# Stick-breaking attention without mask products: GpSimd selects the zeros, scores run ahead of the values

## The chip, the cores and the metric

The kernel runs on one core of one Trainium2 chip, as one launch. The metric is the device time of that launch in microseconds (us); lower is better.

## What is computed

The program is a chain of two transformer blocks on 256 tokens of width 1024, all in float32. Only one layer matters here: the stick-breaking attention of the first block's second layer, with 12 heads of 64 columns. Cut to what matters:

```python
z = einsum("bhqd,bhkd->bhqk", q, k) * scale          # 12 heads, 256 queries, up to 256 keys
mask = key_position < query_position                 # strictly causal
log_not = where(mask, log_sigmoid(-z), 0.0)
later = cumsum(log_not, axis=3, reverse=True) - log_not
wts = where(mask, exp(log_sigmoid(z) + later), 0.0)
out = einsum("bhqk,bhkd->bhqd", wts, v)
```

So the mask is needed twice: masked keys must add nothing to the running sums of log_not (which is minus the softplus of z), and their weights must be zero.

## The kernel before, in words

Every engine has its own instruction list, written by hand; semaphores (`wait_ge`, `then_inc`) order them against each other. TensorE (PE) runs nearly the whole time: most of the program is matmuls of weight matrices that are split into a high and a low part (by ACT at line 489 and DVE at line 966), multiplied in three passes.

The stick-breaking stage works through six **pairs** of heads, p = 0 to 5; the two heads of a pair (e = 0, 1) sit in partitions 0 to 63 and 64 to 127 of the transposed queries `qTB` and keys `kTB`. Everything is held transposed: keys in the partitions, queries in the columns. A head has 384 columns of a PSUM bank: columns 0 to 127 are key block 0 against query block 0, 128 to 255 key block 0 against query block 1, 256 to 383 key block 1 against query block 1. Three sets of two banks (`SB_BANK`) rotate over the pairs. The first and the last of the three blocks are the diagonal ones that need a mask. For one pair the steps are:

1. `sb_scores(p)` on PE. Per head, one product of the identity with `sb_neg_r` (line 2017) writes -1e30 at the masked places of both diagonal blocks and 0 elsewhere; three products of keys and queries of 128 columns each (lines 2022, 2026, 2030) add the scores to it. `sb_neg_r` is a rounded copy of a constant, made once by ACT (line 731).
2. `sb_negated(p)` on DVE (line 1221): -|z| of each head into `sbE`.
3. `sb_softplus(p)` on ACT: Exp (lines 742, 750), then Ln with bias 1 (lines 743, 755), in place in `sbE`.
4. `sb_plus(p)` on DVE (line 1229): max(z, 0) + `sbE` into `sbL`, the softplus; it is 0 at masked places, because z is -1e30 there.
5. `sb_sums(p)` on PE (lines 2038, 2040, 2042): products of `sbL` with a triangle and with ones, added onto the scores in PSUM, head by head. Each head's sums wait for its `sbL`.
6. `sb_weights(p)` on ACT (line 762): one Exp over both heads into `sbW`, the weights; masked places give exp of -1e30, which is 0.
7. `sb_values(p)` on PE (lines 2053, 2056): weights times values; then `sb_hi` on ACT (line 555) and `sb_lo` on DVE (line 1053) split the result into its two parts for the output product.

`sbE`, `sbL` and `sbW` are double buffered (`p % 2`). PE's order is written out by hand:

```python
for p in range(5):
    sb_sums(p)
    if p == 1:
        pe.wait_ge(s_qkd, 3)
    if p:
        sb_values(p - 1)
    if p + 2 < 6:
        sb_scores(p + 2)
```

After it come the first memory logits (line 1841), the sums of pair 5, and then pieces of the output product between the last values. ACT goes, for each p, `sb_softplus(p + 1)`, `sb_weights(p)`, `sb_hi(p - 1)`; DVE goes `sb_plus(p + 1)`, `sb_negated(p + 2)`, `sb_lo(p - 1)`. GpSimd (POOL) has nothing to do in this stage: its work before it is a table of 16 rows near the start, its work after it a DMA that waits for the next feed-forward layer.

Of the kernel before, what the change touches and what calls it, by code (L numbers as in the profile page):

```python
# [15 lines left out]
S = 256  # L16
D = 1024
P = 128
# [68 lines left out]
def build(nc, A):  # L87
# [3 lines left out]
    with ctx:  # L91
        def sem(name):
            return ctx.enter_context(nc.semaphore(name))
# [5 lines left out]
        def place(name, cols, dt=fp32, at=None):  # L99
            if at is None:  # L100
                at = plan["at"]
                plan["at"] += cols
            return nc.alloc_sbuf_tensor_at(name, [P, cols], dt, offset=first + 4 * at)
# [10 lines left out]
        ident_r = place("ident_r", P, f32r)  # L114
# [26 lines left out]
        def over(name, cols):  # L141
# [24 lines left out]
        sbE = over("sbE", 2 * 2 * 384)  # L166
        sbL = over("sbL", 2 * 2 * 384)
        sbW = over("sbW", 2 * 2 * 384)
        sb_neg_r = place("sb_neg_r", 2 * P, f32r, at=cur["at"])
        cur["at"] += 2 * P  # L170
        memPB = over("memPB", 4 * 512)

        cur["at"] = r1
# [27 lines left out]
        s_ohi, s_olo = sem("pair_hi"), sem("pair_lo")  # L201
        s_z, s_abs, s_sbe, s_sbl, s_tri, s_wt, s_sbpv = (sem(n) for n in ("sb_scores", "sb_negated", "sb_log1p",
            "sb_softplus", "sb_summed", "sb_weights", "sb_mixed"))
        s_neg, s_qkd, s_ptd = sem("sb_mask_rounded"), sem("qk_copied_dve"), sem("probsT_copied_dve")
        s_sg, s_hb, s_ht, s_hhi, s_hlo = (sem(n) for n in ("gate_act", "hidden", "hidden_transposed",
                                                         "hidden_hi", "hidden_lo"))
        s_x2p, s_x2h, s_x2, s_gel, s_cmpp, s_cmpc = (sem(n) for n in ("cmp_tokens", "cmp_hi", "cmp_lo",
# [38 lines left out]
        def bank(b, lo=0, hi=512):  # L246
            return ps[:, b, lo:hi]
# [17 lines left out]
            return t[:, (u % NRAW) * UNIT:(u % NRAW + 1) * UNIT]  # L265

        sb_tri, sb_ones = sbc[:, 0:P], sbc[:, P:2 * P]
        sb_neg = sbc[:, 512:1024].rearrange("p (z n) -> p z n", z=2)[:, :, P:2 * P]


        ssq, var, t1, t2 = tiny[:, 0:4], tiny[:, 4:6], tiny[:, 6:8], tiny[:, 208:210]
# [140 lines left out]
        @block.gpsimd  # L412
        def _(pool):
            nc.gpsimd.memset(ident[:, :], 1.0).then_inc(s_idn, 1)
            pool.wait_ge(s_idn, 1)
            nc.gpsimd.affine_select(ident[:, :], ident[:, :], [[1, P]], ALU.is_equal, 0.0, base=0, channel_multiplier=-1)\
                .then_inc(s_idn, 1)
            pool.wait_ge(s_mm, U0["mem_a"])
            pool.dma_start(relT[0:16, :], A["rel_bias_2"].rearrange("n h -> h n"), allow_slow_non_contiguous=True).then_inc(s_tin, 16)
            nc.gpsimd.memset(stage[0:16, 0:512], NEG).then_inc(s_tab, 1)  # L420
            pool.wait_ge(s_tab, 1)
            pool.wait_ge(s_tin, 16)
            for n, (lo, hi) in enumerate(BUCKETS):
                nc.gpsimd.tensor_copy(stage[0:16, TABLE_J0 + lo:TABLE_J0 + hi],
                                      relT[0:16, n:n + 1].broadcast_to([16, hi - lo])).then_inc(s_tab, 1)
            pool.wait_ge(s_tab, 1 + len(BUCKETS))
            pool.dma_start(A["table"], stage[0:16, 0:512]).then_inc(s_tabd, 16)

            pool.wait_ge(s_mm, U0["b_down"] + 1)
            pool.wait_ge(s_hlo, 22)  # L430
            pool.dma_start(gfin[:, :], A["final_norm"].partition_broadcast(P)).then_inc(s_gfin, 16)
            pool.wait_ge(s_mm, U0["b_down"] + 11)

            pool.wait_ge(s_tabd, 16)
            pool.dma_start(strip[:, :].rearrange("p (h c) -> p h c", h=16),
                           bass.AP(A["table"].tensor, 0, [[1, P], [512, 16], [1, 384]])).then_inc(s_strip, 16)
            pool.dma_start(caus[:, :], A["causal"]).then_inc(s_strip, 16)
            for n, kv in enumerate(("k", "v")):
                pool.dma_start(per[16 * n:16 * n + 16, :], A[f"cmp_pe_{kv}_2"].rearrange("(j r) d -> j (r d)", r=2))\
                    .then_inc(s_ind, 16)  # L440
                pool.dma_start(w2[:, HD * n:HD * n + HD], A[f"cmp_w2_{kv}_2"]).then_inc(s_ind, 16)

            def copied(dst, src, step, n):

                s_, d_ = both(front, W_FRONT, src, 1), both(dup, 768, dst, P)
                nc.gpsimd.tensor_copy(d_.rearrange("p t (z n) -> p t z n", n=n),
                                      bass.AP(s_.tensor, s_.offset, [s_.ap[0], s_.ap[1], [step, P // n], [1, n]]))\
                    .then_inc(s_dup, 1)
            pool.wait_ge(s_gact, emptied(G0["front"] + 1, "act"))
            copied(X_KC, C_KC + HD, -HD, HD)  # L450
            copied(X_VC, C_VC + HD, -HD, HD)
            pool.wait_ge(s_gact, emptied(G0["front"] + 2, "act"))
            copied(X_KA, C_KA, 0, HD)
            copied(X_KI, C_KI, 0, 32)
            copied(X_KS, C_KS + HD, -HD, HD)
            pool.wait_ge(s_gact, emptied(G0["front_rest"], "act"))
            copied(X_KW, C_KW + HD, -HD, HD)
            pool.wait_ge(s_sel, 1)
            for h in range(8):
                if h == 6:  # L460
                    pool.wait_ge(s_m, A0["nsa"] + 16)
                for T, (lo, hi) in enumerate(CAUSAL):
                    b0 = 384 * h + TABLE_J0 + 128 * T
                    ins = nc.gpsimd.tensor_tensor(sel_strip(h, lo, hi), strip[:, b0:b0 - (hi - lo):-1], sel[:, lo:hi],
                                                  ALU.add)
                ins.then_inc(s_selb, 1)
            pool.wait_ge(s_mm, U0["down2"] + 1)
            pool.wait_ge(s_hlo, 29)
            pool.dma_start(gfin[:, :], A["norm_final_2"].partition_broadcast(P)).then_inc(s_gfin, 16)
# [3 lines left out]
        def _(act):  # L473
# [253 lines left out]
            act.wait_ge(s_half, HALF["q"] + 1)  # L727
            empty_group(G0["q"], both(qB, D, 0), "b_mix")
            act.preload_act_table_set("natural_log_exp_and_others")
            act.wait_ge(s_sbc, 16)  # L730
            A_(sb_neg_r[:, :].rearrange("p (z n) -> p z n", z=2), sb_neg, ACT.Copy).then_inc(s_neg, 1)
            q_copy(6, ch(qTB, 0, 2), 4, HD ** -0.5)
            act.wait_ge(s_mm, U0["q"] + 4)
            empty_group(G0["q"] + 1, both(qB, D, 512), "b_mix")
# [829 lines left out]
        def _(pe):  # L1564
# [445 lines left out]
            def sb_scores(p):  # L2010

                c = S * p
                if p >= 3:
                    pe.wait_ge(s_wt, p - 2)
                banks = [SB_BANK[p % 3] + e for e in range(2)]
                for e in range(2):
                    MM(bank(banks[e], 0, 512).rearrange("p (z n) -> p z n", z=2)[:, :, 0:P], ident_r[:, :],
                       sb_neg_r[:, :].rearrange("p (z n) -> p z n", z=2), start=True, stop=False,
                       skip_group_check=True)
                for e in range(2):  # L2020
                    r = slice(64 * e, 64 * e + 64)
                    MM(bank(banks[e], 0, P), kTB[r, c:c + P], qTB[r, c:c + P], start=False, stop=False,
                       skip_group_check=True)
                for e in range(2):
                    r = slice(64 * e, 64 * e + 64)
                    MM(bank(banks[e], P, S), kTB[r, c:c + P], qTB[r, c + P:c + S], start=False, stop=False,
                       skip_group_check=True)
                for e in range(2):
                    r = slice(64 * e, 64 * e + 64)
                    MM(bank(banks[e], 256, 384), kTB[r, c + P:c + S], qTB[r, c + P:c + S], start=False, stop=False,  # L2030
                       skip_group_check=True).then_inc(s_z, 1)

            def sb_sums(p):

                for e in range(2):
                    b = SB_BANK[p % 3] + e
                    pe.wait_ge(s_sbl, 2 * p + e + 1)
                    MM(bank(b, 0, 256), sb_tri, sb_half(sbL, p, e, 0, 256), start=False, stop=False,  # L2038
                       skip_group_check=True)
                    MM(bank(b, 128, 256), sb_ones, sb_half(sbL, p, e, 256, 384), start=False, stop=False,  # L2040
                       skip_group_check=True)
                    MM(bank(b, 256, 384), sb_tri, sb_half(sbL, p, e, 256, 384), start=False, stop=True,
                       skip_group_check=True).then_inc(s_tri, 1)

            def sb_values(p):

                o = O0["sb"] + p
                pe.wait_ge(s_wt, p + 1)
                pe.wait_ge(s_olo, o - 1)
                outs = [ps[64 * e:64 * e + 64, OB + o % 2, 0:S] for e in range(2)]  # L2050
                for e in range(2):
# [4 lines left out]
                    ins = MM(outs[e][:, P:S], tok(kvB, 2 * SB, 1)[:, v0:v0 + HD], sb_half(sbW, p, e, 256, 384),  # L2056
                             start=False, stop=True)
                ins.then_inc(s_sbpv, 1)
            pe.wait_ge(s_neg, 1)
            pe.wait_ge(s_idr, 1)  # L2060
            pe.wait_ge(s_qkc, 7)
            sb_scores(0)
            pe.wait_ge(s_qkd, 1)
# [17 lines left out]
            for p in range(5):  # L2081
                sb_sums(p)
                if p == 1:
                    pe.wait_ge(s_qkd, 3)
                if p:
                    sb_values(p - 1)
                if p + 2 < 6:
                    sb_scores(p + 2)
            pe.wait_ge(s_wt, 4)
            mem_logits("mem_b", 0, qTB[:, 6 * S:8 * S], mkTB)  # L2090
            sb_sums(5)
# [451 lines left out]
```

## Time and profile before

| | us |
|---|---|
| median of three runs | 954.84 (954.49 to 955.57) |
| the profiled execution, its own time | 954.67 |
| its span | 953.0 |
| PE busy | 944.5 (99% of the span) |
| DVE busy | 622.1 (65%) |
| ACT busy | 514.6 (54%) |
| POOL busy | 30.7 (3%) |
| TensorE clock, mean share of full speed | 0.999 |

How to read it: the chain of work that ended last is 98% PE, so a microsecond that PE saves or waits is, to first order, a microsecond of the run. The stick-breaking stage lies between 338.5 and some 370 us of the span. A plain float32 product shows as two matmul records (so "x2" on lines 2022 to 2056 is one product), while the mask product of line 2017, in the rounded format, shows as one. Records of neighbouring matmuls overlap; the time that a step takes PE is therefore read from the start of its first record to the start of the next step's first record.

### The profile page before, as it was taken

The page shows a single profiled execution, that of the slowest core. Times are in us where ns is not written, and L with a number is a line of the kernel's source. Part 1 is how long each engine was busy: PE and PEld are TensorE (multiplying, and loading weights), DVE is VectorE, ACT ScalarE, POOL GpSimd, SP SyncE. Part 2 cuts the span into 40 slices and gives each one's busy share as a digit, 9 for nine tenths or more (in the row PEclk, how much of TensorE's full clock was granted, in tenths as well). Part 3 has the DMA queues.
Part 4 walks back from the last instruction along what each step waited for, and adds up shares of the span by engine and source line. Part 5 has one row for each costly group of instructions (what it writes and reads, how often), then busy time and mean ns, then how long its engine had stood idle before and what let it go on. Part 6 is the DMA issues. An engine that isn't in the chain of part 4 may idle for free.

```text
span 953.0 us, 13086 instructions
## 1 busy us (share of the span) xinstructions
PE 944.5 (99%) x5102; PEld 784.9 (82%) x5102; DVE 622.1 (65%) x858; ACT 514.6 (54%) x687; POOL 30.7 (3%) x71
## 2 busy tenths in 40 slices
PE   9999999999999999999999999999999999999997
PEld 6878888888888887888888888877777888888886
DVE  6554877776457366577777447688884776775444
ACT  6754555554346575655555336667685455544333
POOL 0400000000000000000000001000310000000000
PEclk9999999999999999999999999999999999999999
DMA  9715555555555420655555657643224555555561
GB/s 363 234 50 187 189 181 197 196 176 184 215 177 178 175 89 1 221 177 183 202 188 176 220 199 302 220 145 134 89 99 167 177 177 180 189 200 203 188 209 44
DMA packets 25723, 168.66 MB, mean 177 GB/s; under 512 B 2749, under 2 KB 3627, under 8 KB 6475
## 3 DMA queue, kind: packets, MB, share of 16 engines
q1 hardware_dynamic: 24320, 163.39, 48.6%
q0 software_dynamic: 1264, 4.57, 1.2%
q8 instruction: 32, 0.52, 0.2%
q14 instruction: 16, 0.13, 0.0%
q10 hardware_dynamic: 91, 0.04, 0.0%
HBM read 166.91 MB, written 1.08 MB: 176 GB/s over the span
## 4 chain that ended last, share of the span: by engine, by line
PE 98%; DVE 1%; DMA 1%; ACT 0%; issue 0%; SPq 0%; DVEq 0%; ACTq 0%
PE ps L1592 49%; PE ps L1916 23%; PE ps L1919 12%; PE ps L1709 1%; PE ps L2303 1%; PE ps L2313 1%; PE ps L2332 1%; PE ps L1831 1%; PE ps L2038 1%; PE ps L1822 1%; PE ps L1668 1%; DMA raw<-in_in 1%; PE ps L1794 1%; PE ps L1871 0%; PE ps L1841 0%; PE ps L2151 0%
## 5 line engine op out<-in xcount | busy, mean ns | idle before, releaser
L966 DVE TENSOR_TENSOR w_both<-raw,w_both 128x2048 fp32r<-128x2048 f32 x149 | 339.6, 2287 | 157.4 <-ACT w_both L489 157.4
L489 ACT ACTIVATE w_both<-raw 128x2048 fp32r<-128x2048 f32 x149 | 283.4, 1912 | 134.4 <-DMA raw<-in_down 40.9
L1916 PE MATMUL ps<-a_both,w_both 128*128 128x512 f32 x960 | 264.3, 395 | 0.0
L1592 PE MATMUL ps<-w_both,a_both 128*128 128x512 f32 (+1 forms) x816 | 191.0, 388 | 0.0
L1916 PEld LDWEIGHTS ps<-a_both,w_both 128*128 128x128 f32 x960 | 163.3, 189 | 21.2
L1592 PEld LDWEIGHTS ps<-w_both,a_both 128*128 128x128 f32 x816 | 146.8, 188 | 31.1 <-issue 2.6
L1919 PEld LDWEIGHTS ps<-a_both,w_both 128*128 128x128 f32 x960 | 149.0, 189 | 21.5
L1592 PE MATMUL ps<-w_both,h_hi 128*128 128x512 f32 x576 | 154.5, 389 | 0.0
L1919 PE MATMUL ps<-a_both,w_both 128*128 128x256 f32 x960 | 154.5, 281 | 0.0
L1592 PEld LDWEIGHTS ps<-w_both,h_hi 128*128 128x128 f32 x576 | 107.8, 188 | 22.2
L1592 PE MATMUL ps<-w_both,h_lo 128*128 128x512 f32 x288 | 88.7, 389 | 0.0
L666 ACT ACTIVATE mlp_b<-ps 128x1024 f32<-128x1024 f32 x30 | 30.8, 1027 | 102.3 <-PE ps L1919 102.3
L1592 PE MATMUL ps<-w_both,m_hi 128*128 128x512 f32 x256 | 71.5, 400 | 0.0
L1592 PEld LDWEIGHTS ps<-w_both,h_lo 128*128 128x128 f32 x288 | 54.1, 188 | 11.3
L1166 DVE TENSOR_TENSOR mlp_a<-ps,mlp_b 128x1024 f32<-128x1024 f32 x22 | 26.9, 1224 | 55.0 <-ACT mlp_b L666 55.0
L1592 PEld LDWEIGHTS ps<-w_both,m_hi 128*128 128x128 f32 x256 | 46.7, 188 | 10.6 <-issue 1.8
L1592 PE MATMUL ps<-w_both,m_lo 128*128 128x512 f32 x128 | 39.6, 390 | 0.0
L514 ACT ACTIVATE a_both<-ps,gam 128x256 fp32r<-128x256 f32 x48 | 18.9, 476 | 25.4 <-PE ps L1709 25.4
L1592 PEld LDWEIGHTS ps<-w_both,m_lo 128*128 128x128 f32 x128 | 24.0, 188 | 5.3
L1004 DVE SCALAR_TENSOR_TENSOR a_both<-ps,gam,a_both 128x256 fp32r<-128x256 f32 x48 | 20.2, 477 | 9.6 <-ACT a_both L514 9.6
L683 ACT ACTIVATE h_hi<-mlp_a 128x512 f32 (+1 forms) x22 | 14.0, 634 | 19.8 <-DVE mlp_a L1173 19.8
L885 ACT ACTIVATE prob<-prob,tiny 128x128 f32<-128x128 f32 (+1 forms) x48 | 21.3, 454 | 3.8 <-DVE tiny L1425 3.8
(271 smaller groups left out, 762.3 us busy)
## 6 DMA issues: line engine op xcount, KB each, us to landing
raw<-in_a_gu SPq DMA_DIRECT2D x22, 1024.0 KB, 4.7
raw<-in_b_gu SPq DMA_DIRECT2D x22, 1024.0 KB, 4.7
raw<-in_up SPq DMA_DIRECT2D x16, 1024.0 KB, 4.8
raw<-in_down SPq DMA_DIRECT2D x16, 1024.0 KB, 4.8
raw<-in_a_down SPq DMA_DIRECT2D x11, 1024.0 KB, 4.7
raw<-in_b_down SPq DMA_DIRECT2D x11, 1024.0 KB, 4.7
raw<-in_front SPq DMA_DIRECT2D x8, 1024.0 KB, 4.8
raw<-in_gates SPq DMA_DIRECT2D x8, 1024.0 KB, 4.8
```

Source lines behind the costliest of these rows:

```text
L489: A_(ring(w_hi, us)[:, 0:n], ring(raw, us)[:, 0:n], ACT.Copy).then_inc(s_hi, 1)
L514: ins = A_(ch(hi, c), src, ACT.Copy, scale=gam[:, g + c:g + c + 1])
L666: A_(slices(slot(mlp_b, bs % 2)), quad_banks(bs % 2, S, 2 * S), ACT.Copy).then_inc(s_cor, 1)
L683: A_(h_hi[:, bass.ds(512 * bs + 1024 * i, 512)], slot(mlp_a, bs % 2, 512, 1024), ACT.Copy).then_inc(s_hhi, 1)
L885: ins = A_(v, v, ACT.Exp, bias=nmax[e][:, T:T + 1], scale=-1.0, accum_out=rsum[e][:, T:T + 1])
L966: V.tensor_tensor(ring(w_lo, us)[:, 0:n], ring(raw, us)[:, 0:n], ring(w_hi, us)[:, 0:n].bitcast(fp32), ALU.subtract).then_inc(s_lo, 1)
L1004: ins = V.scalar_tensor_tensor(ch(lo, c), src, gam[:, g + c:g + c + 1], h, ALU.mult, ALU.subtract)
L1166: V.tensor_tensor(slices(t), quad_banks(bs % 2, 0, S), slices(c_), ALU.add).then_inc(s_gdve, 1)
L1592: ins = MM(ps[:, b + T, 0:wd], chT(parts[ap_], c, T), wp[wp_][:, off:off + wd], start=(c == first and pn == 0), stop=(c == last and pn == 2))
L1668: ins = MM(bank(4 if i == 2 else 2 * PAIR[g + i] + T, 0, hi - lo), chT(parts[ap_], c, T), ring((w_hi, w_lo)[wp_], U0[name] + j)[:, cols], ...
L1916: MM(bank(4 * k + s).rearrange("p (z n) -> p z n", z=2), ring(w_hi, us)[:, cols[s]], both_parts[:, :, c, :], start=c == 0, stop=False)
L1919: ins = MM(bank(4 * k + s, 0, S), ring(w_lo, us)[:, cols[s]], ch(a_hi, c), start=False, stop=c == KC - 1)
```

## The change

- The mask products, `sb_neg_r`, its ACT copy and its semaphore go. The scores start their banks themselves.
- The first two score products of a head, 128 columns each with the same keys, become one of 256 columns.
- GpSimd gets a new list of 24 selects, two per pair on `sbL` and two per pair on `sbW`, each over the two diagonal blocks of a head (2 x 128 columns): places with key >= query become 0.
- The sums wait for the masked `sbL` (`s_lm`) instead of DVE's `s_sbl`, the values for the masked `sbW` (`s_wm`) instead of ACT's `s_wt`.
- On PE `sb_scores(p + 2)` is put ahead of `sb_values(p - 1)`.

```diff
@@ GpSimd's list, between the table's store and final_norm's load
+            def causal_only(t, p, e):
+
+                v = sb_half(t, p, e)
+                v = bass.AP(v.tensor, v.offset, [v.ap[0], [S, 2], [1, P]])
+                return nc.gpsimd.affine_select(v, v, [[0, 2], [1, P]], ALU.is_gt, 0.0, base=0, channel_multiplier=-1)
+            for p in range(7):
+                for e in range(2 if p else 0):
+                    pool.wait_ge(s_wt, p)
+                    causal_only(sbW, p - 1, e).then_inc(s_wm, 1)
+                for e in range(2 if p < 6 else 0):
+                    pool.wait_ge(s_sbl, 2 * p + e + 1)
+                    causal_only(sbL, p, e).then_inc(s_lm, 1)
@@ ACT's list
-            act.wait_ge(s_sbc, 16)
-            A_(sb_neg_r[:, :].rearrange("p (z n) -> p z n", z=2), sb_neg, ACT.Copy).then_inc(s_neg, 1)
@@ sb_scores(p)
                 for e in range(2):
-                    MM(bank(banks[e], 0, 512).rearrange("p (z n) -> p z n", z=2)[:, :, 0:P], ident_r[:, :],
-                       sb_neg_r[:, :].rearrange("p (z n) -> p z n", z=2), start=True, stop=False,
-                       skip_group_check=True)
-                for e in range(2):
                     r = slice(64 * e, 64 * e + 64)
-                    MM(bank(banks[e], 0, P), kTB[r, c:c + P], qTB[r, c:c + P], start=False, stop=False,
-                       skip_group_check=True)
-                for e in range(2):
-                    r = slice(64 * e, 64 * e + 64)
-                    MM(bank(banks[e], P, S), kTB[r, c:c + P], qTB[r, c + P:c + S], start=False, stop=False,
+                    MM(bank(banks[e], 0, S), kTB[r, c:c + P], qTB[r, c:c + S], start=True, stop=False,
                        skip_group_check=True)
@@ sb_sums(p)
-                    pe.wait_ge(s_sbl, 2 * p + e + 1)
+                    pe.wait_ge(s_lm, 2 * p + e + 1)
@@ sb_values(p)
-                pe.wait_ge(s_wt, p + 1)
+                pe.wait_ge(s_wm, 2 * p + 2)
@@ before the first scores
-            pe.wait_ge(s_neg, 1)
             pe.wait_ge(s_idr, 1)
+            pe.wait_ge(s_sbc, 16)
@@ PE's loop over the pairs
+                if p + 2 < 6:
+                    sb_scores(p + 2)
                 if p:
                     sb_values(p - 1)
-                if p + 2 < 6:
-                    sb_scores(p + 2)
```

On PE, one round of the loop (sums of pair 1, up to the first of pair 2's) stands so before, with `sbL` the sums, `sbW` the values, and `sb_neg_r` and `qTB` the scores:

```order
L2038 MATMUL ps<-sbL,sbc 128x256
L2040 MATMUL ps<-sbL,sbc 128x128
L2042 MATMUL ps<-sbL,sbc 128x128
L2053 MATMUL ps<-sbW,kvB 64x256 x2
L2056 MATMUL ps<-sbW,kvB 64x128 x2
L2017 MATMUL ps<-sb_neg_r,ident_r 128x2x128 x2
L2022 MATMUL ps<-qTB,kTB 128x128 x2
L2026 MATMUL ps<-qTB,kTB 128x128 x2
L2030 MATMUL ps<-qTB,kTB 128x128 x2
L2038 MATMUL ps<-sbL,sbc 128x256
```

and so with the change:

```order
L2037 MATMUL ps<-sbL,sbc 128x256
L2039 MATMUL ps<-sbL,sbc 128x128
L2041 MATMUL ps<-sbL,sbc 128x128
L2025 MATMUL ps<-qTB,kTB 128x256 x2
L2029 MATMUL ps<-qTB,kTB 128x128 x2
L2052 MATMUL ps<-sbW,kvB 64x256 x2
L2055 MATMUL ps<-sbW,kvB 64x128 x2
L2037 MATMUL ps<-sbL,sbc 128x256
```

Eight score instructions of a pair have become four, and they stand ahead of the values. On POOL the list now reads, after the table's store:

```order
L424 DMA distance_table<-stage 16x512
L430 AFFINE_SELECT sbL<-sbL 128x2x128 x2
L430 AFFINE_SELECT sbW<-sbW 128x2x128 x2
L430 AFFINE_SELECT sbL<-sbL 128x2x128 x2
L430 AFFINE_SELECT sbW<-sbW 128x2x128 x2
L430 AFFINE_SELECT sbL<-sbL 128x2x128 x2
```

The rows go on in that alternation to pair 5. The `sbW` row between two `sbL` rows is the earlier pair's: the softplus sums of pair p are selected behind the weights of pair p - 1.

## Rows read from the trace of the kernel before

**Rows 1.** The page's busy line of PE, and busy time by stretch (stretch, its length, busy times).

```profile
PE 944.5 (99%) x5102; PEld 784.9 (82%) x5102; DVE 622.1 (65%) x858; ACT 514.6 (54%) x687; POOL 30.7 (3%) x71
352.00:357.00 5.00, 5.00 (x48) 4.00 (x45) 2.84 (x7) 3.58 (x8) 0.00 (x0) 1.00 0.00 0
```

**Rows 2.** PE's timeline, start of the stage (start us, duration us, engine, line).

```profile
338.50 0.40 PE L2017 MATMUL ps<-sb_neg_r,ident_r 128*128 128x256 f32 x2
...
339.70 0.51 PE L2017 MATMUL ps<-sb_neg_r,ident_r 128*128 128x256 f32 x2
...
342.12 0.70 PE L2038 MATMUL ps<-sbL,sbc 128*128 128x256 f32 x2
```

**Rows 3.** PE's timeline, one round of the loop.

```profile
351.27 0.65 PE L2053 MATMUL ps<-sbW,kvB 128*64 128x256 f32 x4
...
352.07 0.50 PE L2017 MATMUL ps<-sb_neg_r,ident_r 128*128 128x256 f32 x2
352.50 0.49 PE L2022 MATMUL ps<-qTB,kTB 64*128 64x128 f32 x4
...
353.05 0.39 PE L2030 MATMUL ps<-qTB,kTB 64*128 64x128 f32 x4
353.37 0.70 PE L2038 MATMUL ps<-sbL,sbc 128*128 128x256 f32 x2
...
355.32 0.65 PE L2053 MATMUL ps<-sbW,kvB 128*64 128x256 f32 x4
```

**Rows 4.** PE's timeline, end of the stage.

```profile
360.18 1.13 PE L1841 MATMUL ps<-mkTB,qTB 64*128 64x256 f32 x8
361.24 0.70 PE L2038 MATMUL ps<-sbL,sbc 128*128 128x256 f32 x2
...
362.87 0.39 PE L2042 MATMUL ps<-sbL,sbc 128*128 128x128 f32 x2
...
366.98 0.65 PE L2053 MATMUL ps<-sbW,kvB 128*64 128x256 f32 x4
```

**Rows 5.** ACT's timeline (in brackets: idle before, and what ended it).

```profile
340.39 0.53 ACT L742 ACTIVATE sbE<-sbE 128x384 f32<-128x384 f32 x1 [0.42 <-DVE sbE L1221]
...
344.79 0.79 ACT L762 ACTIVATE sbW<-ps 128x768 f32<-128x768 f32 x1
...
363.30 0.82 ACT L762 ACTIVATE sbW<-ps 128x768 f32<-128x768 f32 x1 [0.21 <-PE ps L2042]
```

**Rows 6.** DVE's timeline.

```profile
339.80 1.02 DVE L1221 TENSOR_SCALAR sbE<-ps 128x384 int32<-128x384 int32 x2 [1.79 <-PE ps L2030]
341.50 0.56 DVE L1229 SCALAR_TENSOR_TENSOR sbL<-ps,sbE 128x384 f32<-128x384 f32 x1 [0.68 <-ACT sbE L743]
...
351.44 1.02 DVE L1229 SCALAR_TENSOR_TENSOR sbL<-ps,sbE 128x384 f32<-128x384 f32 x2 [0.67 <-ACT sbE L755]
```

**Rows 7.** POOL's timeline: the start of the program, and a group of copies later.

```profile
0.36 0.10 POOL L2494 MEMSET const-float32-1.0<- 128x1 f32 x1
...
0.82 0.20 POOL L414 MEMSET ident<- 128x128 f32 x1 [0.29 <-POOLq L2494]
1.10 0.29 POOL L416 TENSOR_SCALAR_AFFINE_SELECT ident<-ident 128x128 f32<-128x128 f32 x1
...
614.80 1.09 POOL L446 COPY kvm<-front 128x256 f32<-128x256 f32 x3 [11.24 <-ACT front L574]
```

**Rows 8.** POOL's groups, shapes apart, of all the run and of 614.5 to 615.2 us.

```profile
L424 POOL COPY stage<-relT 16x144 f32<-16x144 f32 x1 | 0.3, 294 | 0.0
L446 POOL COPY kvm<-front 128x256 f32<-128x256 f32 x2 | 0.7, 401 | 11.2 <-ACT front L574 11.2
```

**Rows 9.** POOL's groups of 682 to 683 us, and timeline of DVE and POOL near 622 us.

```profile
L464 POOL TENSOR_TENSOR strip<-strip,sel 128x256 f32<-128x256 f32 x1 | 0.7, 728 | 0.0
...
621.64 2.29 DVE L966 TENSOR_TENSOR w_both<-raw,w_both 128x2048 fp32r<-128x2048 f32 x1 [2.69 <-ACT w_both L489]
...
622.35 1.84 POOL L446 COPY kvm<-front 128x256 f32<-128x256 f32 x1 [6.46 <-ACT front L574]
```

More of the change, by code:

```diff
@@ L168, in build @@
         sbW = over("sbW", 2 * 2 * 384)
-        sb_neg_r = place("sb_neg_r", 2 * P, f32r, at=cur["at"])
-        cur["at"] += 2 * P
         memPB = over("memPB", 4 * 512)
@@ L203, in build @@
             "sb_softplus", "sb_summed", "sb_weights", "sb_mixed"))
-        s_neg, s_qkd, s_ptd = sem("sb_mask_rounded"), sem("qk_copied_dve"), sem("probsT_copied_dve")
+        s_lm, s_wm, s_qkd, s_ptd = sem("sb_sums_masked"), sem("sb_weights_masked"), sem("qk_copied_dve"), sem("probsT_copied_dve")
         s_sg, s_hb, s_ht, s_hhi, s_hlo = (sem(n) for n in ("gate_act", "hidden", "hidden_transposed",
@@ L267, in build @@
         sb_tri, sb_ones = sbc[:, 0:P], sbc[:, P:2 * P]
-        sb_neg = sbc[:, 512:1024].rearrange("p (z n) -> p z n", z=2)[:, :, P:2 * P]
         ssq, var, t1, t2 = tiny[:, 0:4], tiny[:, 4:6], tiny[:, 6:8], tiny[:, 208:210]
```

## The prediction, made before the changed kernel ran

> **What bounds the kernel now.** I read the page's busy times first, then busy time by stretch, then PE's timeline through the stage, and last ACT's, DVE's and POOL's. PE is busy 944.5 of 953.0 us, and in the middle of this stage it is busy in all 5.00 of 5 us while POOL has nothing, at a granted clock of 1.00 of full speed [rows 1]. So the stage costs what PE's instructions cost, and anything that leaves PE waiting is paid in full. One round of the loop, from one pair's values to the next, takes 355.32 - 351.27 = 4.05 us. It is 0.80 of values (351.27 to 352.07), 1.30 of scores (352.07 to 353.37) and 1.95 of sums (353.37 to 355.32) [rows 3]. The softplus sums of the pair after lie ready by then: DVE works on pair 3's `sbL` from 351.44 to 352.46 [rows 6] and PE turns to its sums at 353.37 [rows 3], so 0.9 us or more are spare before.
>
> **What the change takes away.** The two mask products of a pair take 352.50 - 352.07 = 0.43 us of PE; the two 128-column product groups behind them take 353.05 - 352.50 = 0.55 for two heads [rows 3]. What one group of 256 columns costs instead is read from the memory logits, which have the same 64 rows and 256 columns: four of them take 361.24 - 360.18 = 1.06 [rows 4], so two take 0.53, and merging gives 0.02. The last group stays 0.32 [rows 3]. Scores cost 0.85 in place of 1.30: **0.45 a pair, 2.7 us over six**, if PE never waits. ACT's copy of the mask and the wait for it go too; PE enters the stage without idling at 338.50 [rows 2], behind the query product, so that is worth nothing.
>
> **What it adds.** Every `sbL` and `sbW` now passes POOL, which takes its 24 selects strictly in order. A select of two 128-column blocks is not in the trace. The nearest rows: a select of 128 columns took 0.29 [rows 7]; a copy of 144 columns took 0.294 as well, and one of 256 columns 0.401 [rows 8]. So the select goes as the copy does, and I take 0.40 for it. Three such copies one after another took 1.09 us in all [rows 7], a step of (1.09 - 0.40) / 2 = 0.345 and one full 0.40 at the end. Those had no waits between them; here each select has one of its own, already met. That is bounded below by nothing and above by a full hand-over: from DVE's `sbL` (341.50 + 0.56 = 342.06) to PE's sums at 342.12 it took 0.06 [rows 2, 6]. I take 0.03 each. Three selects in a row then cost **D = 1.09 + 0.09 = 1.18**. The bounds of D are 3 x 0.29 less two overlaps of 0.055 (0.401 - 0.345), 0.77, if 256 columns cost no more than 128, and 2 x 0.675 + 0.73 + 0.09 = 2.17 if a select goes as POOL's two-input add of 256 columns, 0.728 [rows 9].
>
> **Where that stands on the path.** POOL's order is: softplus of pair p - 1, weights of p - 1, softplus of p. The weights of p - 1 exist only after the sums of p - 1, and the sums of p now need the softplus selected behind them. That is a new loop: sums(p - 1), ACT's Exp, two selects on `sbW`, one on `sbL`, sums(p). Its length in steps:
> - from the start of a pair's sums to the Exp: 363.30 - 361.24 = 2.06 [rows 4, 5];
> - the Exp 0.82, which is its time when it had been waiting [rows 5];
> - to POOL 0.06, the hand-over above;
> - D = 1.18;
> - from POOL to PE 0.08, the nearest being POOL's wait for itself, 1.10 - (0.82 + 0.20) [rows 7].
>
> Sum 4.20 us a round, where PE has 1.95 + 0.85 + 0.80 = 3.60 to do. The round was 4.05. So each round loses 0.15 where it was to win 0.45, and PE waits 0.60 in it. The second head's `sbL` is selected 0.35 to 0.4 later, and PE needs it about 0.98 after the first (half of the 1.95), so it adds nothing. Putting the scores ahead of the values lets DVE begin 0.80 earlier on a chain that already had room; it costs nothing and gives nothing here, since the values it delays are wanted only by the split for the output product, a long way on.
>
> **The start.** Scores of pair 0 take 0.85 rather than 339.70 - 338.50 = 1.20 [rows 2], so DVE starts at 339.80 - 0.35 = 339.45 [rows 6]. ACT has been free from 340.39 - 0.42 = 339.97 [rows 5], so its first Exp and all of the first softplus come 0.35 earlier: pair 0's `sbL` from DVE at 342.06 - 0.35 = 341.71. With 0.06 + 0.40 + 0.08 it reaches PE at 342.25, 0.13 later than 342.12 [rows 2]. ACT's weights of pair 0 come behind pair 1's softplus, at 344.79 - 0.35 = 344.44 [rows 5] (the sums are done at 342.25 + 2.06 = 344.31), and end at 345.23. The sums of pair 1 start at 345.23 + 0.06 + 1.18 + 0.08 = 346.55, and those of pair 5 four rounds later, at 346.55 + 4 x 4.20 = **363.35**. Before they start at 361.24 [rows 4]. In the last round PE has 1.95 + 0.80 + 1.06 = 3.81, less than 4.20.
>
> **Behind it.** Pair 5's weights from ACT would end 2.88 after the sums' start and be selected a microsecond later; the values want them 366.98 - 361.24 = 5.74 after it [rows 4]. They are hidden. From there PE is saturated as before, so the **2.1 us** stay. The profiled execution took 954.67 (0.17 under the median of 954.84), which gives 956.8 for it and **957.0** against the median. A measurement of this kernel can tell about 0.2%, 1.9 us, from no change: the forecast is slower, by very little more than that.
>
> **A rule of contention weighed.** One copy on POOL took 1.84 us rather than 0.40, from 622.35 to 624.19; DVE's `TENSOR_TENSOR` beside it, with both inputs in SBUF, ran until 623.93 [rows 9]. The DVE instructions in this stage read PSUM, or PSUM and `sbE` [rows 6]. With no blocking D stays; if each round held one such block of 0.5 us (a DVE instruction of this stage), the sum would be 5 x 0.5 = 2.5 higher. The Trainium skill, "SBUF — State Buffer", section "Who interferes with whom", says that a DVE instruction contends with a reading GpSimd instruction only with two SBUF inputs or in a 2-port mode, not with one SBUF input; by that rule, and the row agrees with it, the term is nothing.
>
> **Rivals.**
> - *A select has a small base and a slow element.* A memset of one column took 0.10 [rows 7]; if that were the select's base too, 128 columns in 0.29 mean 1.5 ns each, and 256 cost 0.49: D = 2 x 0.435 + 0.49 + 0.09 = 1.45, and five times 0.27 makes 1.4 more: 958.4. Against it: copies read their input, as selects do, and from 144 to 256 columns they grew by 0.107 only [rows 8]. The Trainium skill, "GPSIMD Engine Reference", section "Performance pitfalls for Q7 kernels", has 2.03 cycles an element for a compare-and-select body and 1.03 when it is unrolled; by the first, with the page's 1.2 GHz, 256 columns would be an estimated 0.51, and the time 958.7. No run here shows which body this is.
> - *Not slower: the loop is there, but its selects are short.* If nearly all of 0.29 is fixed, D = 0.77, a round 3.79, and the end of the stage comes at 346.14 + 3 x 3.79 + 3.81 = 361.3, 0.1 after 361.24: 954.9. With waits that cost nothing D = 1.09, and the time is 957.0 - 5 x 0.09 = 956.5. It decides from D under about 1.14, where five rounds stay under the 1.9 us. For it: the step of 0.345 in a row of copies. Against: 0.401 against 0.294 shows that length counts.
> - *Two-input rate.* D = 2.17: 957.0 + 5 x 0.99 = 962.0. Against: the select has one input.
> - *The loop does not bind, and PE keeps the 2.7 us:* 952.1. It needs POOL to do three selects in about 0.58 us, which no row comes near.
>
> **How the numbers follow.** My forecast 0.52 (956.2 to 957.8; 0.40 of it above the line of 0.2%, at 956.75, and 0.12 below), slow element 0.15, short selects 0.23, two-input rate 0.06, PE keeps its gain 0.04. Slower is 0.40 + 0.15 + 0.06 = 0.61, within 0.2% is 0.12 + 0.23 = 0.35, faster 0.04. The range leaves out the last two cases and goes from the short selects' 954.9, about, to a little over the slow element's 958.4: 954.9 to 958.9.
>
> **What would show it.** In the profile after: selects of some 0.40 us; PE idle of about 0.6 us before the first sums of pairs 2 to 5, ended by POOL, and about 1.5 before pair 1's; a round of 4.2 us; sums of pair 5 near 363.3; the scores' four groups in 0.85. It is wrong if the round is 3.6 (no loop), if the sums are released by DVE's timing rather than by the weights' selects, or if a select takes other than 0.35 to 0.45. If PE's idle time is as I say but the run isn't slower, something behind the stage gave it back.

## The result and the profile after

The changed kernel takes **956.76 us** (median of 20 runs, 956.06 to 957.21) against 954.83 for the kernel before in the same sessions (20 runs, 954.37 to 955.57). Run by run the ratio is 1.0018, with a 95% interval of 1.0012 to 1.0024: slower by 1.1 to 2.3 us. The forecast was 957.0. The profiled execution took 957.21, with a span of 955.5.

PE's timeline after, through the start of the stage and one round of the loop (start us, duration us, engine, line; in brackets the idle time before and what ended it). Lines have moved: 2025 and 2029 are the scores, 2037 to 2041 the sums, 2052 and 2055 the values.

```profile
339.31 0.70 PE L2025 MATMUL ps<-qTB,kTB 64*128 64x256 f32 x4
...
340.06 0.60 PE L2025 MATMUL ps<-qTB,kTB 64*128 64x256 f32 x4
...
343.05 0.70 PE L2037 MATMUL ps<-sbL,sbc 128*128 128x256 f32 x2 [1.15 <-POOL sbL L430]
...
345.10 0.70 PE L2025 MATMUL ps<-qTB,kTB 64*128 64x256 f32 x4
...
347.28 0.70 PE L2037 MATMUL ps<-sbL,sbc 128*128 128x256 f32 x2 [1.26 <-POOL sbL L430]
...
349.23 0.70 PE L2025 MATMUL ps<-qTB,kTB 64*128 64x256 f32 x4
...
350.08 0.65 PE L2052 MATMUL ps<-sbW,kvB 128*64 128x256 f32 x4
350.57 0.39 PE L2055 MATMUL ps<-sbW,kvB 128*64 128x128 f32 x4
351.39 0.70 PE L2037 MATMUL ps<-sbL,sbc 128*128 128x256 f32 x2 [0.44 <-POOL sbL L430]
...
355.50 0.70 PE L2037 MATMUL ps<-sbL,sbc 128*128 128x256 f32 x2 [0.44 <-POOL sbL L430]
...
363.73 0.70 PE L2037 MATMUL ps<-sbL,sbc 128*128 128x256 f32 x2 [0.23 <-POOL sbL L430]
```

Before, PE's timeline had no bracket in the whole stage [rows 2 to 4]. Now the first sums of each pair have one, and each names POOL's select on `sbL`. A round is 355.50 - 351.39 = 4.11 us, where it was 4.05 [rows 3]. Its scores take 350.08 - 349.23 = 0.85, where they were 1.30. PE's own work in a round is 1.95 + 0.85 + 0.80 = 3.60, so 0.45 was saved and 4.11 - 3.60 = 0.51 lost; the bracket shows 0.44 of it, since it counts from the end of the record before.

What stands between two pairs' sums is read on ACT's and POOL's timelines after:

```profile
349.34 0.81 ACT L769 ACTIVATE sbW<-ps 128x768 f32<-128x768 f32 x1 [0.88 <-PE ps L2041]
```

```profile
342.60 0.40 POOL L430 TENSOR_SCALAR_AFFINE_SELECT sbL<-sbL 128x256 f32<-128x256 f32 x1 [294.38 <-DVE sbL L1236]
...
350.21 0.77 POOL L430 TENSOR_SCALAR_AFFINE_SELECT sbW<-sbW 128x256 f32<-128x256 f32 x2 [2.63 <-ACT sbW L769]
350.93 0.76 POOL L430 TENSOR_SCALAR_AFFINE_SELECT sbL<-sbL 128x256 f32<-128x256 f32 x2
```

The sums of pair 1 start at 347.28; the Exp starts at 349.34 (2.06 later) and ends at 350.15; POOL starts on the weights at 350.21 and on the softplus at 350.93; PE starts pair 2's sums at 351.39. DVE had written the softplus of pair 2 well before, both heads from 348.07 to 349.09:

```profile
348.07 1.02 DVE L1236 SCALAR_TENSOR_TENSOR sbL<-ps,sbE 128x384 f32<-128x384 f32 x2 [1.00 <-ACT sbE L762]
```

The first head's lay in SBUF from 348.63 to 350.93, because POOL takes its list in order and stood at a wait for the weights. The waits of PE in the stage, added up, are one row after (engine, line, what it waited for: us, times, longest):

```profile
PE ps L2037 <- POOL sbL L430: 3.9, 6, 1.3
```

From the first scores to the sums of pair 5 it is 363.73 - 339.31 = 24.42 us, where it was 361.24 - 338.50 = 22.74 [rows 2, 4]: 1.68 more. From there to the end nothing changed: 955.5 - 363.73 = 591.77, against 953.0 - 361.24 = 591.76. The profiled execution is 2.5 us longer than that of before; the other 0.81 lies ahead of the stage. In the profiled executions below the stage starts anywhere from 338.36 to 339.27, in no order of the changes, so I take this for scatter of one execution. The medians differ by 1.93 us, of which the stage explains 1.68; that figure lies in the interval of 1.1 to 2.3, and no run says where the 0.25 between them comes from.

The selects themselves, as a group of POOL's from 337 to 372 us after (count, then busy us, mean ns of one, idle time before), took 0.406 each:

```profile
L430 POOL TENSOR_SCALAR_AFFINE_SELECT sbL<-sbL 128x256 f32<-128x256 f32 x12 | 4.6, 406 | 294.9 <-DVE sbL L1236 294.9
```

### The profile page after: what moved, and what is told of

Its sections match the earlier page's. It is cut to its first block, busy times and chain, and to the rows that moved or that the text cites. A ratio compares the mean times of both kernels' runs of the same rounds, so it can differ in the third digit from the quotient of the medians.

```text
span 955.5 us, 13038 instructions
## 1 busy us (share of the span) xinstructions
PE 943.5 (99%) x5066; PEld 783.9 (82%) x5066; DVE 622.4 (65%) x858; ACT 514.2 (54%) x686; POOL 39.7 (4%) x95
## 4 chain that ended last, share of the span: by engine, by line
PE 97%; ACT 1%; DVE 1%; POOL 1%; issue 0%; DVEq 0%
PE ps L1599 49%; PE ps L1923 23%; PE ps L1926 12%; PE ps L1716 2%; PE ps L2302 1%; PE ps L2312 1%; PE ps L2331 1%; PE ps L1838 1%; PE ps L2037 1%; PE ps L1829 1%; PE ps L1732 1%; PE ps L1675 1%; PE ps L1801 1%; PE ps L1878 0%; ACT sbW L769 0%; PE ps L2150 0%
```

## The experiments

In the two theories that stood at the start, A says that PE waits because of the order of POOL's list, B that it waits because the chain from scores to sums has become too long. C doubts the price of the products taken away (of the mask products in one run, of the merged product in another), and D and E are about the start of the stage. "Stage" below is the time from the first scores to the sums of pair 5.

**Softplus selects first.** The same 24 selects, two loops exchanged:

```diff
             for p in range(7):
-                for e in range(2 if p else 0):
-                    pool.wait_ge(s_wt, p)
-                    causal_only(sbW, p - 1, e).then_inc(s_wm, 1)
                 for e in range(2 if p < 6 else 0):
                     pool.wait_ge(s_sbl, 2 * p + e + 1)
                     causal_only(sbL, p, e).then_inc(s_lm, 1)
+                for e in range(2 if p else 0):
+                    pool.wait_ge(s_wt, p)
+                    causal_only(sbW, p - 1, e).then_inc(s_wm, 1)
```

> GpSimd takes the softplus selects of pair p ahead of the weight selects of pair p - 1; all else as in the change. Theory A (the wait is made by GpSimd's order: sums of p - 1, Exp, two weight selects, one softplus select, sums of p): the loop is gone, a round is PE's own 3.60 us, PE idles only before the sums of pair 0 (about 1.15) and pair 1 (about 0.1 to 0.3), and from the first scores to the sums of pair 5 it is 21.4 us, against 24.42 in the change and 22.74 before: 3.0 us faster than the change, 1.3 faster than before, 953.5. Rival B (the latency from the scores through DVE, ACT and GpSimd to the sums is too long whatever the order): rounds stay near 4.1, and the time near 956.8.

Measured: 953.75 us (11 runs, 953.24 to 954.19), ratio to before 0.9988, interval 0.9979 to 0.9997. PE's and POOL's timelines of this run:

```profile
338.36 0.70 PE L2025 MATMUL ps<-qTB,kTB 64*128 64x256 f32 x4
...
342.11 0.70 PE L2037 MATMUL ps<-sbL,sbc 128*128 128x256 f32 x2 [1.15 <-POOL sbL L430]
...
345.20 0.70 PE L2037 MATMUL ps<-sbL,sbc 128*128 128x256 f32 x2
...
348.80 0.70 PE L2037 MATMUL ps<-sbL,sbc 128*128 128x256 f32 x2
...
352.41 0.70 PE L2037 MATMUL ps<-sbL,sbc 128*128 128x256 f32 x2
...
359.83 0.70 PE L2037 MATMUL ps<-sbL,sbc 128*128 128x256 f32 x2
```

```profile
347.76 0.87 POOL L430 TENSOR_SCALAR_AFFINE_SELECT sbL<-sbL 128x256 f32<-128x256 f32 x2 [1.42 <-DVE sbL L1236]
348.58 0.77 POOL L430 TENSOR_SCALAR_AFFINE_SELECT sbW<-sbW 128x256 f32<-128x256 f32 x2
```

The `sbL` selects are now released by DVE, and the weights come behind them. The brackets on PE are gone from pair 1 on; a round is 352.41 - 348.80 = 3.61 and the stage 359.83 - 338.36 = 21.47. Theory A said 3.60 and 21.4; B is out. Pair 2's first select ends at 347.76 + 0.41 = 348.17, 0.63 before PE wants it. With the same products, selects and waits, 3.0 us came from two loops exchanged.

**One more select in the loop.** In the change's order, with a select of the same shape between the two on the weights; its output, into a buffer of its own, is never read:

```diff
                 for e in range(2 if p else 0):
                     pool.wait_ge(s_wt, p)
+                    if e:
+                        pool.wait_ge(s_again, p - 1)
+                        again(p - 1).then_inc(s_again, 1)
                     causal_only(sbW, p - 1, e).then_inc(s_wm, 1)
```

> The change with one more select of the same shape per pair, into a buffer that nobody reads, between the two weight selects. Theory A: it stands in the loop, so each of the rounds into pairs 1 to 5 grows by a select's step, 0.36 to 0.40: 5 x 0.38 = 1.9 us over the change, 958.7, with rounds of 4.5. Rival B (the latency from the scores, where the weight selects are no part of it): no change, 956.8.

Measured: 958.73 us (5 runs, 958.33 to 959.0), 1.97 above the change. PE's timeline of this run, in which lines 2037 and 2049 are the scores and the sums:

```profile
339.27 0.70 PE L2037 MATMUL ps<-qTB,kTB 64*128 64x256 f32 x4
...
352.09 0.70 PE L2049 MATMUL ps<-sbL,sbc 128*128 128x256 f32 x2 [0.80 <-POOL sbL L432]
...
356.56 0.70 PE L2049 MATMUL ps<-sbL,sbc 128*128 128x256 f32 x2 [0.80 <-POOL sbL L432]
...
365.52 0.70 PE L2049 MATMUL ps<-sbL,sbc 128*128 128x256 f32 x2 [0.59 <-POOL sbL L432]
```

A round is 4.47, 0.36 more, and the stage 26.25, 1.83 more than the change's 24.42: five rounds of one select's step, as A has it.

**The same extra select, off the path.** The same lines in the kernel with the softplus selects first.

> The same additional select with the softplus selects first. Theory A: the weight selects are off the path, so it costs nothing: the same as the run with the softplus selects first, 953.5, within 0.3. Rival B or any theory in which GpSimd's busy time as such is the limit: 1.5 to 2 us more than that run.

Measured: 953.8 us (11 runs, 953.08 to 954.27), against 953.75 without it. POOL's groups in this run, from 336 to 370 us (count, then busy us and mean ns):

```profile
L439 POOL TENSOR_SCALAR_AFFINE_SELECT sb_spare<-sbW 128x256 f32<-128x256 f32 x6 | 2.5, 409 | 0.0
```

PE's first scores and its sums of pair 5:

```profile
338.86 0.70 PE L2037 MATMUL ps<-qTB,kTB 64*128 64x256 f32 x4
...
360.33 0.70 PE L2049 MATMUL ps<-sbL,sbc 128*128 128x256 f32 x2
```

The stage is 21.47, as without the extra selects. So 2.5 us of POOL cost nothing here, and 1.97 us of time in the run above. It is the place in the list that has a price, not POOL's time.

**No selects.** This kernel masks nothing: keys at and after the query count like the others.

```diff
-            for p in range(7):
...
-                    pe.wait_ge(s_lm, 2 * p + e + 1)
+                    pe.wait_ge(s_sbl, 2 * p + e + 1)
-                pe.wait_ge(s_wm, 2 * p + 2)
+                pe.wait_ge(s_wt, p + 1)
```

> The change without any select: nothing is masked, keys at and after the query count like the others; DVE's softplus and ACT's weights go to PE directly. Theory A: rounds of 3.60 and, since the first softplus reaches PE some 0.47 earlier, about 21.0 from the first scores to the sums of pair 5: 953.1, some 0.4 under the run with the softplus selects first. This is all that taking the mask products away could give; 2.7 would show only if PE did not idle at the start. Rival C (a mask product costs PE less than its 0.2 us between other products): the round stays above 3.8 and the time above 954.0.

Measured: 953.2 us (11 runs, 952.66 to 953.66), ratio 0.9981, interval 0.9972 to 0.999. PE's timeline of this run:

```profile
338.85 0.70 PE L2018 MATMUL ps<-qTB,kTB 64*128 64x256 f32 x4
...
342.12 0.70 PE L2030 MATMUL ps<-sbL,sbc 128*128 128x256 f32 x2 [0.67 <-DVE sbL L1229]
...
345.21 0.70 PE L2030 MATMUL ps<-sbL,sbc 128*128 128x256 f32 x2
...
348.82 0.70 PE L2030 MATMUL ps<-sbL,sbc 128*128 128x256 f32 x2
...
352.42 0.70 PE L2030 MATMUL ps<-sbL,sbc 128*128 128x256 f32 x2
...
359.85 0.70 PE L2030 MATMUL ps<-sbL,sbc 128*128 128x256 f32 x2
```

A round is 3.60, so rival C is out, and the stage is 21.00, 1.74 under before. Even with no masking at all only that much of the 2.7 us of products shows. From the sums of pair 1 to those of pair 5 the saving is whole: 359.85 - 345.21 = 14.64 against 361.24 - 345.26 = 15.98, 1.34 for the scores of pairs 3 to 5. At the start little of it shows: the sums of pair 0 come 3.27 after the first scores for 3.62 before, and those of pair 1 another 3.09 after for 3.14, so 0.40 shows of the 1.35 of pairs 0 to 2. Before, PE did mask products there in time in which it now mostly waits for softplus sums. The selects with the softplus first cost 21.47 - 21.00 = 0.47 against this run, all of it at pair 0, whose sums come 3.75 after the first scores.

The one row of before that this needs is the sums of pair 1:

```profile
345.26 0.70 PE L2038 MATMUL ps<-sbL,sbc 128*128 128x256 f32 x2
```

**Values first, in the change's order of selects.** Only PE's loop goes back to the old order:

```diff
-                if p + 2 < 6:
-                    sb_scores(p + 2)
                 if p:
                     sb_values(p - 1)
+                if p + 2 < 6:
+                    sb_scores(p + 2)
```

> The change with the old order of PE in its loop: values of p - 1, then scores of p + 2. Theory A: the loop through the weight selects does not pass the scores, so nothing moves: rounds of 4.11, the same as the change within 0.3, 956.7. Rival B (the chain from the scores to the sums counts): each round some 0.8 longer in that chain, so 1 to 3 us slower.

Measured: 956.63 us (11 runs, 956.24 to 957.03), the change's 956.76 within the scatter. PE's timeline of this run has the same bracket and the same round, 354.95 - 350.84 = 4.11:

```profile
350.84 0.70 PE L2037 MATMUL ps<-sbL,sbc 128*128 128x256 f32 x2 [0.44 <-POOL sbL L430]
...
354.95 0.70 PE L2037 MATMUL ps<-sbL,sbc 128*128 128x256 f32 x2 [0.44 <-POOL sbL L430]
```

**Values first, softplus selects first.** The same exchange, on the first experiment.

> The softplus selects ahead of the weight selects, and PE's old order of values and scores. Now the chain from the scores is the longest left: scores end 0.8 later, and by the durations of the change's trace (negation 1.0, two Exp and two Ln 1.85, max and add 0.56, select 0.40, hand-overs 0.3) the softplus of pair p + 2 would still reach PE about 0.5 before it is wanted. Theory A: the same as the run with the softplus selects first, 953.8 within 0.4. Rival B: rounds over 3.7 and a time above 954.5.

Measured: 953.89 us (11 runs, 953.53 to 954.32), against 953.75. PE's sums of pairs 2, 3 and 5 in this run:

```profile
349.33 0.70 PE L2037 MATMUL ps<-sbL,sbc 128*128 128x256 f32 x2
...
352.93 0.70 PE L2037 MATMUL ps<-sbL,sbc 128*128 128x256 f32 x2
...
360.35 0.70 PE L2037 MATMUL ps<-sbL,sbc 128*128 128x256 f32 x2
```

and POOL's selects on the softplus of pair 3:

```profile
352.08 0.87 POOL L430 TENSOR_SCALAR_AFFINE_SELECT sbL<-sbL 128x256 f32<-128x256 f32 x2 [2.21 <-DVE sbL L1236]
```

There is no bracket from pair 1 on and a round is 3.60; with the first scores at 338.88 in this execution the stage is 21.47, as with the scores first. Pair 3's first select ends at 352.08 + 0.41 = 352.49, 0.44 before PE's sums at 352.93, where some 0.5 was expected. So the order of scores and values, the last item of the change, is worth nothing in either order of the selects.

**The merge alone.** The kernel before, with its mask products, and one score product of 256 columns for two of 128:

```diff
-                    MM(bank(banks[e], 0, P), kTB[r, c:c + P], qTB[r, c:c + P], start=False, stop=False,
-                       skip_group_check=True)
-                for e in range(2):
-                    r = slice(64 * e, 64 * e + 64)
-                    MM(bank(banks[e], P, S), kTB[r, c:c + P], qTB[r, c + P:c + S], start=False, stop=False,
+                    MM(bank(banks[e], 0, S), kTB[r, c:c + P], qTB[r, c:c + S], start=False, stop=False,
                        skip_group_check=True)
```

> The kernel before, mask products kept, with only the two 128-column score products of a head merged into one of 256. By the term of the prediction a merge gives 0.02 us a pair, 0.1 in all: no change, 954.8. Rival C (behind other products a group of 256 columns costs 0.43, as the change's second scores did, and not 0.53): 0.1 a pair, a round of 3.94, 0.6 us in all: 954.3.

Measured: 954.74 us (11 runs, 954.33 to 955.38), ratio 0.9999, interval 0.999 to 1.0008. PE's timeline of this run:

```profile
352.52 0.50 PE L2017 MATMUL ps<-sb_neg_r,ident_r 128*128 128x256 f32 x2
352.96 0.70 PE L2022 MATMUL ps<-qTB,kTB 64*128 64x256 f32 x4
353.49 0.39 PE L2026 MATMUL ps<-qTB,kTB 64*128 64x128 f32 x4
353.81 0.70 PE L2034 MATMUL ps<-sbL,sbc 128*128 128x256 f32 x2
```

The merged group takes 353.49 - 352.96 = 0.53 behind the mask products, against 0.55 for the two groups [rows 3]. The time alone would not part 954.8 from C's 954.3 (the interval holds both), but the group's 0.53 for C's 0.43 does: C is out. Of the 0.45 that a pair's scores save, the mask products are 0.43.

**Scores of pair 2 early.** On the first experiment, to see whether PE's 1.15 us of idle time before pair 0's sums can be filled:

```diff
             b_round(7, q_left + 1)()
+            sb_scores(2)
...
-                if p + 2 < 6:
+                if 0 < p and p + 2 < 6:
                     sb_scores(p + 2)
```

> The softplus selects first, and PE takes the scores of pair 2 before the sums of pair 0, where it idles 1.15 us, rather than after them. Theory D (what is left at the start is the latency of the softplus of pairs 0 and 1 on DVE, ACT and GpSimd, not PE's work): the idle time moves from before the sums of pair 0 to before those of pair 1, which start where they did or up to 0.15 earlier, and the time stays at 953.8, at most 0.2 less. Rival E (PE's idle time at the start is free to be filled): 0.8 us less, 953.0.

Measured: 953.66 us (11 runs, 953.16 to 953.8), against 953.75: D, not E's 953.0. PE's timeline of this run:

```profile
338.64 0.70 PE L2025 MATMUL ps<-qTB,kTB 64*128 64x256 f32 x4
...
342.38 0.70 PE L2037 MATMUL ps<-sbL,sbc 128*128 128x256 f32 x2 [0.29 <-POOL sbL L430]
...
345.47 0.70 PE L2037 MATMUL ps<-sbL,sbc 128*128 128x256 f32 x2 [0.98 <-POOL sbL L430]
```

The idle time moved from pair 0 to pair 1 and did not shrink: pair 1's sums start 345.47 - 338.64 = 6.83 after the first scores, with 345.20 - 338.36 = 6.84 in the first experiment. What bounds the start is the softplus of pairs 0 and 1 on its way through DVE, ACT and POOL. Starting that chain earlier, inside the query product, was not tried.

## Why the prediction was right

- **The loop through POOL.** It was forecast from the order of the list alone, as the one thing that decides, and the first three experiments show it: exchange the loops and it is gone, lengthen it and each round grows by that much, do the same work beside it and nothing grows.
- **Its length.** Forecast 4.20, measured 4.11. The Exp started 2.06 after the sums, as said, and took 0.81 for 0.82. Three selects in a row took 351.34 - 350.21 = 1.13 (the softplus select starts at 350.93, two steps of 0.36 on, and takes 0.41), where D was 1.18: the 0.03 for a wait that is already met was too much, it is about 0.015 by the difference to the copies' step. From POOL to PE it took 0.05, not 0.08. Four such rounds, and 0.08 at pair 1's sums, are the 0.43 us by which the stage came out shorter than forecast: 24.42, not 363.35 - 338.50 = 24.85. Before pair 5's sums PE idled only 0.23, less than the 0.6 that the signs name for pairs 2 to 5: the last round has 3.81 of work in it, as the prediction's own sum says.
- **The select.** 0.40 by the copy of 256 columns, 0.406 measured. The rival with the slow element (0.49) falls: with 0.294 for 128 columns the added 128 cost 0.11, under 0.9 ns each. The two-input rate (0.73) falls too. The rival with short selects falls in its first form, a select of 0.29. Its second form, waits that cost nothing (D = 1.09, 956.5), came nearly true: D was 1.13, just under the 1.14 at which that rival set the border to a change within 0.2%. The Trainium skill's "GPSIMD Engine Reference", section "Performance pitfalls for Q7 kernels", has 1.03 and 2.03 cycles an element for such a body; at the 1.2 GHz that the prediction took from that page, 0.112 us for 128 columns are an estimated 1.05 cycles each, which agrees with the lower figure, not with 2.03.
- **What was taken away.** Scores 0.85 a pair for 1.30 in the loop, exact (pair 0's took 340.06 - 339.31 = 0.75, which changed nothing, since PE waited there); the merge's 0.02 was borne out by the seventh experiment. Pair 0's softplus reached PE 343.05 - 339.31 = 3.74 after the first scores, forecast 3.75; pair 1's sums came 7.97 after them, forecast 8.05.
- **No contention.** All 24 selects took 0.40 to 0.41, also those beside DVE's negations (350.18 to 351.20) and, in the first experiment, beside its softplus sums (347.13 to 348.15), so the term that was set to nothing is nothing. These DVE instructions have none or one of their inputs in SBUF. The trace agrees here with what the Trainium skill's "SBUF — State Buffer", section "Who interferes with whom", says of DVE instructions with one SBUF input.
- **Behind the stage** the time did not change (591.77 against 591.76), so the whole of it stayed, as forecast.
- **Where it was close.** The forecast put 0.61 on slower by over 0.2% and 0.35 on within it. The medians are 0.20% apart, the ratio run by run is 0.18%, and its interval, 0.12% to 0.24%, has the line in it: the mechanism held, the side of the line stayed open. The two small surcharges named above are what put the forecast over it: without them the sum gives 956.5. That the median lies as near to 957.0 as to 956.5 is luck, since the 0.25 us that lift it over the stage's own 1.68 have no place in the sum. What bears the mechanism out is the round of 4.11 and the releases, not the total.

## What to carry to other kernels

When work moves to an idle engine, its busy time does not tell what the move costs; write down its list and ask, for each instruction that the critical engine waits for, what stands in front of it and what that waits for. Here a softplus that was ready 2 us early stood behind weights that came out of the previous pair's sums, and exchanging two loops turned a change of +1.9 us into one of -1.2 against the kernel before. A filler for idle time helps only if the engine, and not the latency of its inputs, sets the next start.

## What the runs showed of the hardware beyond the forecast

A wait on POOL that is already met hardly costs: selects with such a wait each followed one another at 0.36 us, copies without waits at 0.345 [rows 7, 8]. The step of 0.36 holds for three and for four selects in a row (the extra select made a round 0.36 longer). That the difference of 0.015 is the wait's price is an estimate; selects without waits were not run. Hand-overs with POOL were as short as between the other engines: 0.06 us from ACT to POOL (350.15 to 350.21), 0.08 from DVE to POOL (341.96 + 0.56 = 342.52 to 342.60), and 0.05 from POOL to PE (351.34 to 351.39).
